# Moving the token-major copy of x from TensorE to VectorE and DMA in a two-layer pooling/SSD trunk

## The chip, the cores and the metric

The kernel runs on one core of one Trainium2 chip. The metric is the device time of one execution in microseconds (us). The kernel before took 1106.39 us, the median of three runs (1106.36 to 1106.46). The engines are TensorE (PE in the rows; PEld is its weight load), VectorE (DVE), ScalarE (ACT), GpSimd (POOL) and SyncE (SP, which issues most DMAs).

## The reference, cut to what matters

The trunk is layer 0 (pooling mixer, then a squared-ReLU MLP) and layer 1 (Mamba-2 SSD mixer, then an MLP), for 512 tokens of width 1024, all float32. The change touches the SSD mixer alone, in the part after the input projection and the causal convolution:

```python
xbc = silu(causal_dwconv(xbc, conv_w, conv_b))      # x: 2048 channels, B and C: 4 groups x 128
dt  = softplus(dt_raw + dt_bias)                    # 32 heads, 8 per group
xdt   = x * dtc[..., None]                          # chunks of 128 tokens, 64 channels per head
a_cs  = cumsum(dtc * a)
decay = exp(where(causal, a_cs[l] - a_cs[s], -inf))
cb    = einsum("bclgn,bcsgn->bcgls", cc, bc)
y_diag = einsum("bcgls,bcgrls,bcsgrp->bclgrp", cb, decay, xdt)
states = einsum("bclgn,bcgrl,bclgrp->bcgrpn", bc, exp(a_cs[-1] - a_cs), xdt)
h[c+1] = h[c] * exp(a_cs[-1]) + states[c]
y_off  = einsum("bclgn,bcgrpn,bcgrl->bclgrp", cc, h, exp(a_cs))
y = y_diag + y_off + d_skip * x                     # then * silu(z), group RMSNorm, out projection
```

The sums over tokens (`y_diag`, `states`) need x with the tokens on the partitions ("token-major"), while the projection and the convolution leave it with channels on the partitions ("feature-major").

## The kernel before

Activations live in SBUF feature-major, as tiles of 128 channels x 512 tokens. Weights come from HBM in units of 128 x 1024 (512 KB). A unit passes four stages. SP loads it into `w_raw` (`load_weights`). ACT rounds it to fp32r as `w_hi` (`round_half`, line 445). POOL subtracts to get `w_lo` (`split_half`, line 729). PE multiplies eight 128x128 tiles with 512 tokens, each as three fp32r products in `three` (lines 857 to 859: hi*hi, hi*lo, lo*hi). Every buffer is doubled, so unit u+2 is rounded and split while unit u is multiplied.

The SSD mixer is a table of "slots", one unit each. Six slots produce the convolved tiles of group 0. Then come ten slots for each group g: t = 0 to 3 compute the gate z of group g, and t = 4 to 9 the convolved tiles of group g+1 (B, C, then four tiles of x). The last group uses its later slots for the output projection. Three PSUM banks take turns as accumulators, so slot a starts only when DVE has drained slot a-3. Between the slots the SSD work of group g is placed by hand:

- After t = 1 `token_major` turns B round (4 transposes, line 1016), makes C*B (line 1025) and turns the x of chunks 0 to 2 round (12 transposes, line 1007). Chunk 3 follows after t = 2 (4 transposes). DVE multiplies each by dt out of PSUM (`token_x`, line 1348).
- After t = 3, 5, 7, 9 `chunk` computes chunks 0 to 3: `y_diag` (line 1048), for chunks 1 to 3 `y_off` (line 1057), and for chunks 0 to 2 the state product `states`, again as three fp32r products.
- ACT forms the exponent of a chunk in `exp_segments` (eight Relus, line 634, and an Exp, line 637), at t = 1, 2, 4, 6. DVE multiplies it by C*B into `m` (`decay_times_cb`, line 1364).
- POOL makes the decayed x (`decayed`, line 788) at t = 2, 4, 6. ACT rounds it (`decayed_hi`, line 626) and POOL takes the rest (`decayed_lo`, line 797). POOL also sums squares of the group before (`group_sum`, line 806).
- The convolution of a tile is `conv_scale` (DVE), `first_tap` (ACT) and three taps on DVE (`conv_taps`, line 1278).

The order on each engine is the order of the code; semaphores tie the engines together. The per-head cumulated sums a_cs go through a DRAM scratch once (line 383) and come back broadcast to 128 partitions, one chunk at a time (`load_acs`), all on the SP queue.

Of the kernel before, what the change touches and what calls it, by code (L numbers as in the profile page):

```python
# [6 lines left out]
F32 = mybir.dt.float32  # L7
# [4 lines left out]
P = 128  # L12
# [44 lines left out]
T_TOKEN, T_LATE_TOKEN = 1, 2  # L57
# [37 lines left out]
def build(nc, xt, x_tok, pooling, weights, dt_weights, params, consts, out_first, out_second):  # L95
    ctx = ExitStack()
    with ctx:
# [52 lines left out]
        bt_hi, _ = sb("b_token_hi", [P, CHUNKS, P], F32R)  # L150
        bt_hi_f = bt_hi[:, :, :].bitcast(F32)
        cbm, _ = sb("cb_masked", [P, CHUNKS, P])
        dec, o_dec = sb("x_dt_decayed", [P, TOK])
        dec_lo, _ = sb("x_dt_decayed_lo", [P, TOK], F32R, o_dec)
        dec_hi, _ = sb("x_dt_decayed_hi", [P, TOK], F32R)
        dec_hi_f = dec_hi[:, :].bitcast(F32)
# [7 lines left out]
        ex, o_ex = sb("dt_exp", hd4)  # L164
# [5 lines left out]
        bt_lo, _ = sb("b_token_lo", [P, CHUNKS - 1, P], F32R, o_ex)  # L170
# [18 lines left out]
        acs_dram = nc.dram_tensor("acs_scratch", [GROUPS, CHUNKS, HPG, P], F32).ap()  # L189
        eacs_dram = nc.dram_tensor("eacs_scratch", [GROUPS, CHUNKS, HPG, P], F32).ap()  # L190
# [5 lines left out]
        XT_BANK = (b_yd, b_yo, b_st, b_misc)  # L196
# [60 lines left out]
        x_mm = sem("x_transposed")  # L257
# [3 lines left out]
        bt_lo_ready = sem("b_token_lo_ready")  # L261
        dec_ready = sem("dec_ready")
        dec_hi_ready = sem("dec_hi_ready")
        dec_lo_ready = sem("dec_lo_ready")
# [59 lines left out]

        def conv_out(n):

            g, q = divmod(n, CONVS)
            return bf[:, :] if q == 0 else cf[:, g % 2, :] if q == 1 else xact[:, q - 2, :]
# [5 lines left out]
        def _(sp):  # L334
# [42 lines left out]
            for u in range(5):  # L377
                load_ahead(u)
            sp.wait_ge(acsf_ready, 1)
# [6 lines left out]
            load_ahead(5)  # L386
            sp.wait_ge(scratch, 2 * GROUPS * 16)
# [44 lines left out]
        def _(act):  # L432
# [142 lines left out]

            for u in range(CONVS):
# [5 lines left out]
                if u == 5:  # L582
# [4 lines left out]
                    act.activation(eacs_f[:, :], acs_f[:, :], ACT.Exp).then_inc(decays, 1)  # L587
                first_tap(u)
# [6 lines left out]
            def silu_b_c(g):  # L595

                for q in range(2):
# [3 lines left out]
            def silu_x(g):  # L601
                act.wait_ge(acc_drained, A_SSM + conv_slot(CONVS * g + CONVS - 1) + 1)
                act.activation(xact[:, :, :], xact[:, :, :], ACT.Silu).then_inc(x_act, 1)

            def skip(g):

                act.wait_ge(x_act, g + 1)
# [10 lines left out]
            def b_token(g):  # L618
                act.wait_ge(bt_mm, g + 1)
                act.activation(bt_hi[:, :, :], b_misc[:, :].rearrange("p (c n) -> p c n", c=CHUNKS),  # L620
                               ACT.Copy).then_inc(bt_ready, 1)

            def decayed_hi(g, c):

                act.wait_ge(dec_ready, 3 * g + c + 1)
                act.activation(dec_hi[:, :], dec[:, :], ACT.Copy).then_inc(dec_hi_ready, 1)
# [29 lines left out]
            for g in range(GROUPS):  # L656
                ends = g == GROUPS - 1
                for t in range(slots(g)):
                    u = slot_of(g, t)
                    if t == 2:  # L660
                        decayed_hi(g, 0)
                    ahead(u, 0)
                    if t == 0:
                        silu_b_c(g)
                        silu_x(g)
# [11 lines left out]
                    if t in (4, 6):  # L677
                        decayed_hi(g, (t - 2) // 2)
                    if not ends and t >= GT:
                        first_tap(CONVS * (g + 1) + t - GT)  # L680
                    if t == 0:
                        skip(g)
                    if t == 1 and g:
# [5 lines left out]
                    if t in FALL_IN:  # L689
# [32 lines left out]
        def _(pool):  # L722
# [60 lines left out]
            def decayed(g, c):  # L783

                pool.wait_ge(xdt_ready, 4 * g + c + 1)
                if g or c:
                    pool.wait_ge(st_ready, 3 * g + c)
                pool.tensor_tensor(
                    dec[:, :].rearrange("p (h d) -> p h d", h=HPG),
# [3 lines left out]

            def decayed_lo(g, c):

# [857 lines left out]
```

## Time and profile before

| | before |
|---|---|
| median of three runs | 1106.39 us |
| profiled execution, its own time | 1106.54 us |
| profiled execution, first to last instruction (span) | 1104.7 us |
| PE busy | 1092.8 us (99%) |
| PE weight loads | 899.8 us (81%) |
| DVE, ACT, POOL busy | 577.3, 474.2, 610.8 us |
| granted TensorE clock | 0.998 of full |
| mean DMA traffic | 106 GB/s |

The busy time of an engine covers the whole span, and a matmul's end is modelled: successive matmuls overlap in the rows. So what a matmul costs is read as the distance from its start to the start of the next one. The SSD part runs from about 386 us to 700 us in the trace.

### The profile page before, as it was taken

The numbers are of one execution on the slowest core, as the hardware profiler recorded it, in microseconds if no ns is written. First come the engines' busy times: TensorE is split into PE (matmuls) and PEld (weight loads), VectorE is DVE, ScalarE is ACT, GpSimd is POOL, SyncE is SP. The second block draws the span as 40 slices with busy tenths as digits, with TensorE's granted clock in tenths as the row PEclk, the third lists the DMA queues.
The fourth block names the chain that finished last, engine by engine and source line by source line (L and its number), as shares of the span: only waits on it lengthen the run. The fifth ranks groups of instructions, "written<-read, shape, count | busy, mean of one in ns | idle before, by whom it ended". The sixth has DMA issues, their size and how long they took to land.

```text
span 1104.7 us, 15384 instructions
## 1 busy us (share of the span) xinstructions
PE 1092.8 (99%) x5168; PEld 899.8 (81%) x5168; DVE 577.3 (52%) x644; ACT 474.2 (43%) x816; POOL 610.8 (55%) x460
## 2 busy tenths in 40 slices
PE   9999999999999999999999999999999999999997
PEld 7788888888888788888887888888888888888886
DVE  5665421455432384676777866666664124554123
ACT  7433222233333338458595785343332222333332
POOL 3866544444566635537466376656665444445653
PEclk9999999999999999999999999999999999999999
DMA  7223232222222225333334233222222222333232
GB/s 286 79 99 105 86 103 97 96 95 95 96 95 95 96 77 152 123 112 124 117 104 143 105 125 106 96 95 96 95 95 96 95 95 95 97 99 101 93 104 77
DMA packets 40085, 117.05 MB, mean 106 GB/s; under 512 B 4080, under 2 KB 11888, under 8 KB 40048
## 3 DMA queue, kind: packets, MB, share of 16 engines
q1 hardware_dynamic: 39616, 115.83, 31.3%
q10 hardware_dynamic: 432, 0.73, 0.2%
q8 instruction: 22, 0.36, 0.1%
q14 instruction: 15, 0.12, 0.0%
HBM read 114.32 MB, written 2.23 MB: 105 GB/s over the span
## 4 chain that ended last, share of the span: by engine, by line
PE 93%; ACT 2%; DVE 1%; POOL 1%; issue 1%; DMA 1%; ACTq 0%; DVEq 0%; POOLq 0%
PE bank L857 30%; PE bank L859 29%; PE bank L858 29%; PE bank L1048 1%; PE bank L1057 1%; DMA params<-params 1%; ACT m L634 1%; PE bank L898 1%; PE bank L1007 0%; ACT w_hi L445 0%; POOL w_lo L729 0%; POOL residual L756 0%; PE bank L878 0%; PE bank L1025 0%; ACT y_accumulated L609 0%
## 5 line engine op out<-in xcount | busy, mean ns | idle before, releaser
L729 POOL TENSOR_TENSOR w_lo<-w_raw,w_hi 128x512 fp32r<-128x512 f32 x372 | 497.5, 1343 | 442.5 <-ACT w_hi L445 429.9
L445 ACT ACTIVATE w_hi<-w_raw 128x512 fp32r<-128x512 f32 x372 | 230.5, 626 | 383.0 <-PE bank L859 373.5
L857 PE MATMUL bank<-x_hi,w_hi 128*128 128x512 f32 x848 | 331.9, 391 | 1.8 <-DVE x_lo L1159 1.5
L859 PE MATMUL bank<-x_hi,w_lo 128*128 128x512 f32 x848 | 330.2, 389 | 0.0
L858 PE MATMUL bank<-x_lo,w_hi 128*128 128x512 f32 x848 | 330.1, 389 | 0.0
L857 PE MATMUL bank<-act_hi,w_hi 128*128 128x512 f32 (+1 forms) x656 | 252.9, 386 | 0.0
L859 PE MATMUL bank<-act_hi,w_lo 128*128 128x512 f32 (+1 forms) x656 | 251.8, 384 | 0.0
L858 PE MATMUL bank<-act_lo,w_hi 128*128 128x512 f32 (+1 forms) x656 | 251.8, 384 | 0.0
L857 PEld LDWEIGHTS bank<-x_hi,w_hi 128*128 128x128 f32 x848 | 159.2, 188 | 37.5 <-issue 2.8
L859 PEld LDWEIGHTS bank<-x_hi,w_lo 128*128 128x128 f32 x848 | 159.2, 188 | 33.1
L858 PEld LDWEIGHTS bank<-x_lo,w_hi 128*128 128x128 f32 x848 | 159.3, 188 | 32.6
L857 PEld LDWEIGHTS bank<-act_hi,w_hi 128*128 128x128 f32 x656 | 123.3, 188 | 24.9 <-POOL w_lo L729 0.5
L858 PEld LDWEIGHTS bank<-act_lo,w_hi 128*128 128x128 f32 x656 | 123.3, 188 | 24.8 <-issue 0.5
L859 PEld LDWEIGHTS bank<-act_hi,w_lo 128*128 128x128 f32 x656 | 123.2, 188 | 24.3
L1246 DVE TENSOR_TENSOR tmp<-bank,rstd 128x512 f32<-128x512 f32 x30 | 20.8, 692 | 223.8 <-PE bank L859 223.8
L1231 DVE TENSOR_TENSOR tmp<-tmp 128x512 f32<-128x512 f32 x64 | 115.4, 1804 | 2.2
L548 ACT ACTIVATE act_hi<-tmp 128x512 f32 x64 | 40.5, 632 | 122.6 <-DVE tmp L1231 122.6
L1228 DVE TENSOR_SCALAR tmp<-bank 128x512 f32<-128x512 f32 x64 | 44.3, 692 | 82.5 <-PE bank L859 82.5
L1235 DVE TENSOR_TENSOR act_lo<-tmp,act_hi 128x512 f32 x64 | 46.0, 719 | 60.0 <-ACT act_hi L548 60.0
L745 POOL TENSOR_TENSOR square_sum<-square_sum,squares 128x512 f32<-128x512 f32 x31 | 47.8, 1542 | 32.5 <-ACT squares L452 32.5
L1249 DVE TENSOR_TENSOR residual<-residual,tmp 128x512 f32 x30 | 51.1, 1703 | 4.6 <-DVE tmp L1246 2.4
L1278 DVE SCALAR_TENSOR_TENSOR x_conv<-bank,params,x_conv 128x511 f32<-128x511 f32 (+2 forms) x48 | 35.9, 749 | 18.8 <-ACT x_conv L572 17.7
(161 smaller groups left out, 725.8 us busy)
## 6 DMA issues: line engine op xcount, KB each, us to landing
w_raw<-weights SPq DMA_DIRECT2D x186, 512.0 KB, 3.3
m<-acs_scratch SPq DMA_DIRECT2D x16, 512.0 KB, 4.4
decay_in<-eacs_scratch SPq DMA_DIRECT2D x24, 128.0 KB, 3.8
x_token<-x_tok SPq DMA_DIRECT2D x4, 512.0 KB, 6.4
residual<-xt SPq DMA_DIRECT2D x8, 256.0 KB, 10.1
out_first<-scaled_residual SPq DMA_DIRECT2D x4, 256.0 KB, 2.4
out_second<-output_rows SPq DMA_DIRECT2D x4, 256.0 KB, 2.7
pooling_matrices<-pooling ACTq DMA_DIRECT2D x2, 288.0 KB, 5.2
```

The costliest lines, as they stand in the source:

```text
L445: act.activation(whi[:, c % 2, part], raw[:, c % 2, part], ACT.Copy).then_inc(hi_ready, 1)
L548: act.activation(act_hi[:, bass.ds(2 * i + e, 1), :], tmp[:, e:e + 1, :], ACT.Copy).then_inc(hid_hi_ready, 1)
L729: pool.tensor_tensor(wlo[:, c % 2, part], raw[:, c % 2, part], whi_f[:, c % 2, part], ALU.subtract).then_inc(lo_ready, 1)
L745: pool.tensor_tensor(ssq[:, :], ssq[:, :], sq[:, slot, :], ALU.add).then_inc(ssq_added, 1)
L857: pe.matmul(out, wh, xh, start=start, stop=False)
L858: pe.matmul(out, wh, xl, start=False, stop=False)
L859: return pe.matmul(out, wl, xh, start=False, stop=stop)
L1228: dve.tensor_scalar(tmp[:, e, :], acc[(a - a0 + first) % 2][:, :], 0.0, None, ALU.max).then_inc(acc_drained, 1)
L1231: dve.tensor_tensor(tmp[:, e, :], tmp[:, e, :], tmp[:, e, :], ALU.mult).then_inc(hid_sq_ready, 1)
L1235: dve.tensor_tensor(act_lo[:, tile, :], tmp[:, e:e + 1, :], act_hi_f[:, tile, :], ALU.subtract).then_inc(hid_lo_ready, 1)
L1249: dve.tensor_tensor(h[:, tile, :], h[:, tile, :], tmp[:, e:e + 1, :], ALU.add).then_inc(h_done, 1)
L1278: dve.scalar_tensor_tensor(out=out[:, back:], in0=p[:, 0:TOK - back], scalar=col("conv_w", 24 * k + n), in1=out[:, back:], op0=ALU.mult, o ...
```

## The change

Five things change.

1. x becomes token-major without PE. DVE transposes 32x32 blocks of the four activated x tiles (`transpose_blocks`, four instructions per group) into the free part of `y_accumulated`. SP writes them to a DRAM scratch in four DMAs (`write_blocks`) and reads them back in one (`read_tokens`). DVE multiplies by dt from there in two halves per chunk (`token_x`). PE's 16 transposes of x per group, and the waits around them, are gone.
2. The state product is one plain float32 matmul of `b_token` and `x_dt_decayed`. `decayed_hi` (ACT), `decayed_lo` (POOL) and `b_token_lo` (DVE) are gone, and the decayed x has two buffers.
3. The convolved tiles come in the order x, B, C. The Silu of x moves to t = 8 of the group before (for group 0 to the fifth of the first six slots), that of B and C stays at t = 0. `skip` moves from t = 0 to t = 3.
4. ACT's exponent of chunk 0 stands in front of `group_squares`.
5. DVE's x_dt and m of chunk 0 stand in front of the gate's drain at t = 2. Those of chunks 1 to 3 follow it.

The diff, cut:

```diff
-        dec, o_dec = sb("x_dt_decayed", [P, TOK])
...
+        dec, _ = sb("x_dt_decayed", [P, 2, TOK])
+        x_dram = nc.dram_tensor("x_scratch", [GROUPS, CHUNKS * (P // Q), Q, P // Q, GT * Q], F32).ap()
...
+            def write_blocks(g):
+                sp.wait_ge(xt_blocks, g + 1)
+                blocks = x_blocks(g)
+                for a in range(P // Q):
+                    sp.dma_start(x_dram[g, :, :, a, :].rearrange("n q f -> q n f"),
+                                 blocks[Q * a:Q * a + Q, :, :]).then_inc(xt_written, 16)
+            def read_tokens(g):
+                sp.wait_ge(xt_written, 16 * (P // Q) * (g + 1))
+                sp.dma_start(yx[:, GT * g:GT * g + GT, :],
+                             x_dram[g].rearrange("(c b) q a f -> (b q) c (a f)", c=CHUNKS)
+                             ).then_inc(xt_landed, 16)
...
+            write_blocks(0)
             sp.wait_ge(acsf_ready, 1)
             sp.wait_ge(decays, 3)
...
             load_ahead(5)
+            read_tokens(0)
             sp.wait_ge(scratch, 2 * GROUPS * 16)
...
+                    if t == 8 and g + 1 < GROUPS:
+                        write_blocks(g + 1)
+                    if t == 9 and g + 1 < GROUPS:
+                        read_tokens(g + 1)
...
+                if u == 4:
+                    silu_x(0)
...
-                act.wait_ge(x_act, g + 1)
+                act.wait_ge(xdt_ready, 4 * g + 4)
                 for i in range(GT):
...
+                    if not ends and t == 8:
+                        silu_x(g + 1)
                     ahead(u, 0)
...
-            def token_x(g, c):
-                for i in range(GT):
-                    last = pe.transpose(XT_BANK[c][:, P * i:P * i + P], xact[:, i, P * c:P * c + P], ident)
-                last.then_inc(x_mm, 1)
...
-                    three(b_st[:, :], bt_hi[:, c, :], bt_lo[:, c, :], dec_hi[:, :], dec_lo[:, :], True, True
-                          ).then_inc(st_ready, 1)
+                    pe.matmul(b_st[:, :], bt[:, c, :], dec[:, c % 2, :], start=True, stop=True).then_inc(st_ready, 1)
...
+            def transpose_blocks(g):
+                dve.wait_ge(x_act, g + 1)
+                blocks = x_blocks(g)
+                for i in range(GT):
+                    last = dve.transpose(blocks[:, :, Q * i:Q * i + Q],
+                                         xact[:, i, :].rearrange("p (n j) -> p n j", j=Q))
+                last.then_inc(xt_blocks, 1)
...
                 conv_scale(u)
+                if u == 4:
+                    transpose_blocks(0)
                 conv_taps(u)
...
+                dve.wait_ge(xt_landed, 16 * (g + 1))
+                out = xdt[:, c, :].rearrange("p (i h a j) -> p h i a j", h=2, a=2, j=Q)
+                landed = yx[:, GT * g + c, :].rearrange("p (h a i j) -> p h i a j", h=2, a=2, j=Q)
+                dt = dt_t[:, c, HPG * g:HPG * g + HPG].rearrange("p (i h) -> p h i", h=2)
+                for half in range(2):
+                    last = dve.tensor_tensor(out[:, half], landed[:, half],
+                                             dt[:, half].unsqueeze(2).unsqueeze(3).to_broadcast([P, GT, 2, Q]),
+                                             ALU.mult)
```

The order of ACT (names: `m` holds the exponents, `squares` the squares of the group before, `x_dt_decayed_hi` the rounded decayed x), from the Silu at t = 0 of group 2 on. Before:

```order
L599 ACTIVATE b_feature<-b_feature 128x512
L599 ACTIVATE c_feature<-c_feature 128x512
L603 ACTIVATE x_conv<-x_conv 128x2048
L616 ACTIVATE z_silu<-z_silu 128x2048
L445 ACTIVATE w_hi<-w_raw 128x512
L609 ACTIVATE y_accumulated<-x_conv,params 128x512 x4
L445 ACTIVATE w_hi<-w_raw 128x512 x2
L642 ACTIVATE squares<-y_accumulated 128x512 x4
L620 ACTIVATE b_token_hi<-bank 128x512
L634 ACTIVATE m<-m,cumulated 128x128 x8
```

And now, the same place:

```order
L625 ACTIVATE b_feature<-b_feature 128x512
L625 ACTIVATE c_feature<-c_feature 128x512
L638 ACTIVATE z_silu<-z_silu 128x2048
L465 ACTIVATE w_hi<-w_raw 128x512 x3
L651 ACTIVATE m<-m,cumulated 128x128 x8
L654 ACT_TABLE_LOAD
L654 ACTIVATE m<-m 128x1024
L659 ACTIVATE squares<-y_accumulated 128x512 x4
L642 ACTIVATE b_token<-bank 128x512
```

The Silu of x and the four skip products have left this place, and the exponent stands ahead of the squares.

The order of POOL at t = 2 of group 1 to 3 (`square_sum` is the sum over the group before, `x_dt_decayed` the decayed x of a chunk). Before:

```order
L788 TENSOR_TENSOR x_dt_decayed<-x_dt,decay_to_end 128x512
L806 TENSOR_TENSOR square_sum<-squares 128x512
L806 TENSOR_TENSOR square_sum<-square_sum,squares 128x512 x2
L797 TENSOR_TENSOR x_dt_decayed_lo<-x_dt_decayed,x_dt_decayed_hi 128x512
L729 TENSOR_TENSOR w_lo<-w_raw,w_hi 128x512 x3
```

And now:

```order
L817 TENSOR_TENSOR square_sum<-squares 128x512
L817 TENSOR_TENSOR square_sum<-square_sum,squares 128x512 x2
L745 TENSOR_TENSOR w_lo<-w_raw,w_hi 128x512
L804 TENSOR_TENSOR x_dt_decayed<-x_dt,decay_to_end 128x512
L745 TENSOR_TENSOR w_lo<-w_raw,w_hi 128x512
```

The decayed x of chunk 0 now stands behind the three sums and a half of a weight unit.

The order of the SP queue at the start of group 0 (`m` and `decay_in` are the broadcast loads of the exponents, `x_scratch` is the new DRAM scratch) is now:

```order
L338 DMA w_raw<-weights 128x1024 x5
L363 DMA x_scratch<-y_accumulated 32x16x128 x4
L398 DMA acs_scratch<-a_cs_feature 8x4x128
L398 DMA eacs_scratch<-exp_a_cs_feature 8x4x128
...
L338 DMA w_raw<-weights 128x1024
L369 DMA y_accumulated<-x_scratch 128x4x512
L345 DMA m<-acs_scratch 128x1024 x2
L355 DMA decay_in<-eacs_scratch 64x4x128 x4
```

Before, the rows with `x_scratch` were not there; now the loads of `m` stand behind the writes and the read of x.

## Rows read from the trace of the kernel before

**Rows 1.** The page: busy time of each engine, share of the span, instructions.

```profile
PE 1092.8 (99%) x5168; PEld 899.8 (81%) x5168; DVE 577.3 (52%) x644; ACT 474.2 (43%) x816; POOL 610.8 (55%) x460
```

**Rows 2.** Waits of PE: engine, line, releaser; us in total, times, longest.

```profile
PE bank L1048 <- DVE m L1364: 1.0, 1, 1.0
```

**Rows 3.** Timeline of PE after t = 1 of group 0: start, duration, instruction.

```profile
429.44 1.47 PE L1007 MATMUL bank<-constants,x_conv 128*128 128x128 f32 x12
430.67 0.48 PE L857 MATMUL bank<-x_hi,w_hi 128*128 128x512 f32 x1
```

**Rows 4.** Timeline of PE at chunk 0 of group 0.

```profile
442.24 1.09 PE L1048 MATMUL bank<-m,x_dt 128*64 128x128 f32 x16
443.26 0.50 PE L857 MATMUL bank<-x_dt_decayed_hi,b_token_hi 128*128 128x512 f32 x1
...
443.83 0.39 PE L859 MATMUL bank<-x_dt_decayed_hi,b_token_lo 128*128 128x512 f32 x1
444.06 0.40 PE L857 MATMUL bank<-x_hi,w_hi 128*128 128x512 f32 x1
444.30 0.39 PE L858 MATMUL bank<-x_lo,w_hi 128*128 128x512 f32 x1
```

**Rows 5.** Timeline of PE at a plain float32 product of the same shape.

```profile
116.68 1.02 PE L878 MATMUL bank<-square_sum,constants 128*128 128x512 f32 x2
117.77 0.39 PE L858 MATMUL bank<-act_lo,w_hi 128*128 128x512 f32 x1
```

**Rows 6.** The chain that ended last, around that product: start, us, what.

```profile
116.84 0.86 PE bank L878 x2
```

**Rows 7.** Timeline of ACT, t = 0 to 2 of group 2.

```profile
559.71 1.90 ACT L603 ACTIVATE x_conv<-x_conv 128x2048 f32<-128x2048 f32 x1
563.83 2.56 ACT L609 ACTIVATE y_accumulated<-x_conv,params 128x512 f32<-128x512 f32 x4
567.33 2.18 ACT L642 ACTIVATE squares<-y_accumulated 128x512 f32<-128x512 f32 x4
569.89 2.44 ACT L634 ACTIVATE m<-m,cumulated 128x128 f32<-128x128 f32 x8
572.35 1.28 ACT L637 ACT_TABLE_LOAD   x1
573.64 1.06 ACT L637 ACTIVATE m<-m 128x1024 f32<-128x1024 f32 x1
```

**Rows 8.** Timeline of ACT, t = 4 of group 2.

```profile
587.38 0.63 ACT L626 ACTIVATE x_dt_decayed_hi<-x_dt_decayed 128x512 fp32r<-128x512 f32 x1 [2.01 <-POOL x_dt_decayed L788]
```

**Rows 9.** Timeline of DVE before group 0: taps of the fourth convolved tile.

```profile
411.53 2.32 DVE L1278 SCALAR_TENSOR_TENSOR x_conv<-bank,params,x_conv 128x511 f32<-128x511 f32 x3 [0.84 <-ACT x_conv L572]
```

**Rows 10.** Timeline of SP at the start of group 0.

```profile
424.45 3.29 SPq L356 DMA_DIRECT2D decay_in<-eacs_scratch  x4
```

**Rows 11.** The page, DMA issues: KB each, median us from issue to landing.

```profile
m<-acs_scratch SPq DMA_DIRECT2D x16, 512.0 KB, 4.4
```

**Rows 12.** Timeline of POOL, t = 2 of group 2.

```profile
570.02 1.05 POOL L788 TENSOR_TENSOR x_dt_decayed<-x_dt,decay_to_end 128x512 f32<-128x512 f32 x1
571.02 1.30 POOL L806 TENSOR_TENSOR square_sum<-squares 128x512 f32<-128x512 f32 x1
572.47 2.73 POOL L806 TENSOR_TENSOR square_sum<-square_sum,squares 128x512 f32<-128x512 f32 x2
```

**Rows 13.** Timeline of PE at chunk 0 of group 2.

```profile
577.26 1.09 PE L1048 MATMUL bank<-m,x_dt 128*64 128x128 f32 x16
```

**Rows 14.** Timeline of DVE, taps of the tile of t = 8, group 2.

```profile
622.31 2.32 DVE L1278 SCALAR_TENSOR_TENSOR x_conv<-bank,params,x_conv 128x511 f32<-128x511 f32 x3 [0.85 <-ACT x_conv L572]
```

**Rows 15.** Timeline of PE, first unit after chunk 3 of group 2.

```profile
621.09 0.48 PE L857 MATMUL bank<-x_hi,w_hi 128*128 128x512 f32 x1
```

**Rows 16.** DVE lines of the SSD part: count, busy us, mean ns, idle before.

```profile
L1348 DVE TENSOR_TENSOR x_dt<-bank,dt_token 128x512 f32<-128x512 f32 x16 | 10.2, 678 | 0.0
```

**Rows 17.** The line of m on DVE: shortest, median and longest duration in ns.

```profile
L1364 DVE TENSOR_TENSOR m<-m,cb_masked x16: 1216/1748/2306, 437.0 to 676.5; 128x1024 f32<-128x1024 f32 x16
```

More of the change, by code:

```diff
@@ L56 @@
 TIMES_CB_IN = {4: 1, 6: 2, 8: 3}
-T_TOKEN, T_LATE_TOKEN = 1, 2
+T_TOKEN = 1
+Q = 32
 T_STAT, T_NORM = 4, 7
@@ L574, in first_tap, with silu_x @@
                                ).then_inc(tap_ready, 1)
+            def silu_x(g):
+                act.wait_ge(acc_drained, A_SSM + conv_slot(CONVS * g + GT - 1) + 1)
+                act.activation(xact[:, :, :], xact[:, :, :], ACT.Silu).then_inc(x_act, 1)
             for u in range(CONVS):
@@ L595, in silu_b_c @@
             def silu_b_c(g):
-                for q in range(2):
+                for q in range(GT, CONVS):
                     act.wait_ge(acc_drained, A_SSM + conv_slot(CONVS * g + q) + 1)
                     act.activation(conv_out(CONVS * g + q), conv_out(CONVS * g + q), ACT.Silu).then_inc(bc_act, 1)
-            def silu_x(g):
-                act.wait_ge(acc_drained, A_SSM + conv_slot(CONVS * g + CONVS - 1) + 1)
-                act.activation(xact[:, :, :], xact[:, :, :], ACT.Silu).then_inc(x_act, 1)
             def skip(g):
-                act.wait_ge(x_act, g + 1)
+                act.wait_ge(xdt_ready, 4 * g + 4)
                 for i in range(GT):
@@ L664, in _ @@
                         silu_b_c(g)
-                        silu_x(g)
                         if g:
@@ L688, in _ @@
                         root(SSM_STAT + g - 1, group_root)
-                    if t in FALL_IN:
+                    if t in FALL_IN and t > 1:
                         exp_segments(g, FALL_IN[t])
@@ L820, in _ @@
                     u = slot_of(g, t)
+                    if t == 2 and g:
+                        group_sum(g - 1)
+                    split_half(U_SSM + u + 2, 0)
                     if t == 2:
                         decayed(g, 0)
-                    if t == 2 and g:
-                        group_sum(g - 1)
-                    if t == 2:
-                        decayed_lo(g, 0)
-                    split_half(U_SSM + u + 2, 0)
-                    if t in (4, 6):
-                        decayed(g, (t - 2) // 2)
                     if t == T_STAT - 1 and g:
@@ L834, in _ @@
                     split_half(U_SSM + u + 2, 1)
-                    if t in (4, 6):
-                        decayed_lo(g, (t - 2) // 2)
+                    if t == 2:
+                        decayed(g, 1)
+                    if CHUNK_AFTER.get(t - 1) == 0:
+                        decayed(g, 2)
                     if g == GROUPS - 1 and t == 10:
@@ L1027, in token_major @@
                 last.then_inc(cb_mm, 1)
-                pe.wait_ge(x_act, g + 1)
-                if g == 0:
-                    pe.wait_ge(acsf_ready, 1)
-                else:
-                    pe.wait_ge(y_add, 4 * g)
-                    pe.wait_ge(y_dec, 3 * g)
-                    pe.wait_ge(state_ready, 3 * g)
-                for c in range(CHUNKS - 1):
-                    token_x(g, c)
             def c_chunk(g, c):
@@ L1044, in chunk @@
                 pe.wait_ge(xdt_ready, 4 * g + c + 1)
-                if c:
+                if g == 0 and c == 0:
+                    pe.wait_ge(acsf_ready, 1)
+                else:
                     pe.wait_ge(y_add, 4 * g + c)
```

86 lines of the change are left out of this document (33 added, 53 removed).

## The prediction

> **What bounds the kernel now.** I read the page's engine times first: TensorE is busy for 1092.8 us, 99% of the span, and no other engine passes 610.8 us [rows 1]. So time goes only where TensorE's own work shrinks or one of its few waits goes, and it comes back wherever a new wait reaches TensorE. Next the waits of TensorE: inside the SSD part there is one of a size that counts, 1.0 us, for DVE's m [rows 2]. It falls at chunk 2 of group 2. Then the timelines of the places that the change touches, for what an instruction costs on TensorE, and those of ACT, POOL, DVE and SP around them, for the slack that the moved work has. The reader is to see in them that matmuls follow each other every 0.23 us (443.83 to 444.06 [rows 4]), so a unit of 24 products is 24 x 0.23 = 5.5 us.
>
> **TensorE's transposes of x.** Twelve in a row take 430.67 - 429.44 = 1.23 us [rows 3], 0.103 us each. Each group has 16, so 1.64 us per group and 4 x 1.64 = 6.6 us in all. They stand on TensorE's own queue, so all of it comes off the path. Leaving and entering fp32r for the four late ones may add 0.1 us.
>
> **The state product, 12 times.** Before, from the first of the three fp32r products to the second product of the next unit: 444.30 - 443.26 = 1.04 us [rows 4]. The plain float32 product of the same shape, to the same point: 117.77 - 116.68 = 1.09 us [rows 5]. That is 0.05 us more. The other side: its two passes take 0.86 us [rows 6] against 3 x 0.23 = 0.69, so 0.17 more. 12 times gives 0.6 to 2.0 us of loss; I take the middle, 1.3, since the one example has a switch of number format at its head that this place doesn't have.
>
> **The old wait.** TensorE's 1.0 us for m [rows 2] was the end of an overloaded ACT: in t = 0 and 1 it did the Silu of x (1.90), the skip products (2.56) and the squares (2.18) ahead of the exponent (2.44 + 1.28 + 1.06) [rows 7], and at t = 4 it stood still 2.01 us until POOL had a decayed x for it to round [rows 8]. That rounding is gone and the exponent is first. I take the 1.0 us as gone. What is late next on that chain is DVE's m itself, and it has at least that microsecond of room.
>
> **ACT, DVE and POOL work that goes** (rounding, remainders) lies beside TensorE and is worth nothing by itself. What is added: four DVE transposes per group. The trace has none; the nearest rows are DVE operations over 512 columns, three taps in 2.32 us, 0.77 each [rows 9], and the product out of PSUM, 0.68 [rows 16]. Lower end 0.6, upper end by the factor that m shows between its shortest and longest case, 2306/1216 = 1.9 [rows 17], so 1.5. I take 0.75, 3.0 us per group.
>
> **New wait 1: the start of group 0.** The chain is now: taps of the fourth tile end at 411.53 + 2.32 = 413.85 [rows 9]. Silu of x 1.90 [rows 7]: 415.8. Four transposes 3.0: 418.8. Four writes of 512 pieces of 512 bytes each: four loads of 256 such pieces took SP 3.29 us [rows 10], so 3.3 to 6.6; I take 5: 423.8. Landing: 4.4 us is the median of a 512 KB load [rows 11], for 256 KB I take 3 (2 to 4.4): 426.8. SP waits for that in front of the read. Behind it stand the read of x (1 MB) and the load of m for chunk 0: 1.0 to issue, 4.4 to land [rows 11], some 3 for the megabyte ahead of it: 435.2. The exponent: 2.44 + 1.28 + 1.06 = 4.8 [rows 7]: 440.0. DVE's m: 1.2 to 2.3, median 1.75 [rows 17]: 441.7. TensorE wants it at 442.24 - 1.64 = 440.6 [rows 4]. So it waits 1.1 us. With the low ends it waits nothing, with the high ends (1.6 + 1.4 + 0.6 more, and 0.75 more for transposes) some 5 us. I take 1.0. The weight unit queued behind the read has the same delay and the same cover.
>
> **New wait 2: chunk 0 of groups 1 to 3.** TensorE's state product there waits for POOL's decayed x. It now stands behind three sums (1.30 + 2.73) and a half unit (about 1.3, as the first sum), then 1.05 for itself [rows 12]. ACT's squares begin about where they did: 4.8 later for the exponent, 1.90 + 2.56 earlier for Silu and skip [rows 7], so at 567.33 + 0.3 = 567.6. The sums can start after two of the four, at 568.7, and POOL is through at 568.7 + 4.0 + 1.3 + 1.05 = 575.1. TensorE gets to it at 577.26 - 1.64 + 1.0 = 576.6 [rows 13]. There is 1.5 us of room. But [rows 17] shows DVE operations that take 1.1 us longer than their like, and if POOL's share such delays three times, the room turns into 1.8 us of wait. I take 0.4 each, 1.2 in all (0 to 5.4).
>
> A rule bears on this. DVE's x_dt was a product out of PSUM, at 0.678 us in the mean and with no idle time [rows 16], while m, with two SBUF inputs, ranges up to 2.3 us [rows 17]. The Trainium skill, "SBUF — State Buffer", section "SBUF: two separate sides", says that a DVE operation with two SBUF inputs and a GpSimd operation lock each other out for the whole instruction. By that rule the trace agrees for m, and the change makes x_dt such an operation too; this is a rival below.
>
> **Cover 3: the tile of t = 8 in groups 1 and 2.** Its taps end at 622.31 + 2.32 = 624.6 [rows 14]. The slot that needs its bank is the second after chunk 3: 621.09 + 5.5 = 626.6 [rows 15]. The room is 2.0 us and the transposes stand ahead of the taps with 3.0. But the old lateness of ACT (2.01 us [rows 8]) that pushed this stretch of DVE is gone, so I cost it at nothing. With transposes of 1.5 us it would be 6.0 - 4.0 = 2.0 us of wait, or 4.0 if ACT's lateness gives nothing back, twice.
>
> **Cover 4: the SP queue in groups 1 to 3.** At t = 8 SP stands until the transposes are done and then issues the writes, at t = 9 it stands until they have landed. Queued behind are the weight unit of t = 9 and the loads of m and decay_in. A unit is rounded two slots after the one that frees its buffer, 11.0 us; less 4.4 to land leaves 6.6 against a delay of about 5. Hidden, with 1.6 us to spare.
>
> **The sum.** -6.6 + 1.3 - 1.0 + 1.0 + 1.2 = -4.1 us. The profiled execution took 1106.54 us by its own time (1104.7 of it span), the median of the runs is 1106.39, the same within 0.15. 1106.4 - 4.1 = 1102.3 us.
>
> A second rule gives another number for new wait 1. The Trainium skill, "DMA: Bandwidth & Descriptors", section "Anatomy of one DMA — SWDGE (gpsimd) path", puts a DMA at about 2.0 us plus its bytes at 436 GB/s. By it a megabyte is 4.4 us each way (an estimate from that page), the chain is some 5 us shorter, TensorE doesn't wait in group 0, and the sum would be 1101.3.
>
> **Rivals.**
> - No new wait. The slack covers everything: -6.6 + 1.3 - 1.0 = -6.3, so 1100.1 us. For it: [rows 12, 13] leave 1.5 us, and both DVE and POOL lose work. Against it: four places would all have to hold, each with under 2 us. Chance 0.2.
> - The way through DRAM is long. Writes in 512-byte pieces issue and land at their high ends, and m of group 0 comes 3 to 4 us later than I take it: 1102.3 + 3.5 = 1105.8 us, within 0.2% of before. For it: four loads of half the pieces held SP for 3.29 us [rows 10]. Against it: x has more than ten microseconds before it is used, and only group 0 has m behind it. Chance 0.15.
> - The shared port. The eight half products of x_dt per group each wait for POOL, and POOL for them, as m does by up to 1.1 us [rows 17]. POOL's decayed x is then late by 1.8 us in three groups, 5.4 instead of 1.2, and m of chunk 0 loses its room too: 1102.3 + 4.2 = 1106.5 us. By the skill's rule above this is the outcome. Against it: the halves of chunks 1 to 3 stand behind the drain, where nobody is near to waiting. Chance 0.1.
> - DVE becomes the bound, the case on the other side. The transposes take 1.5 us each, 6.0 us instead of 3.0 at t = 8, in the stretch where DVE already runs behind TensorE [rows 14, 15]. Then +3.0 at the start of group 0, 4.0 twice at t = 8, and the late B and C and x_dt push chunk 0 by 1.8 instead of 0.4 three times: 3.0 + 8.0 + 4.2 = 15.2, 1102.3 + 15.2 = 1117.5 us. It decides once new waits pass 1.0 + 1.2 + 4.1 = 6.3 us, so with transposes of about 1.1 us already. For it: nothing in this trace has their price. Chance 0.12.
>
> **How the numbers follow.** The forecast has 0.4, the rivals 0.2, 0.15, 0.1 and 0.12; 0.03 is left. 0.2% is 2.2 us, about what a measurement of this kernel can tell from no change: faster is below 1104.2, slower above 1108.6. Faster: 0.37 of the forecast, the 0.2, and 0.11 from the low ends of the next two: 0.68. Same: 0.03 + 0.14 = 0.17 and 0.02 of the last: 0.19. Slower: 0.13. The range runs from 1099.3 (all covers hold and the state product costs only 0.6, -7.0) to 1107.0, which takes in the DRAM and the port cases and leaves out the DVE case.
>
> **What would show it.** TensorE's transposes of x gone and its weight loads 64 fewer. The float32 state product at 0.86 in the chain. The wait of m at chunk 2 of group 2 gone. A wait of the products with m at chunk 0 of group 0 near 1 us, with m's DMA as what ACT waits for. Waits of the state product for POOL's decayed x, 0.4 us each, in groups 1 to 3. DVE's transposes near 0.75 us. The prediction is wrong if a transpose takes over 1.1 us, if TensorE waits for weights behind a standing SP queue, or if the plain state product costs more than 1.1 us from start to next start.

## The result: slower, 1114.52 us

The changed kernel took 1114.52 us in the median of 4 runs (1112.19 to 1115.36), against 1106.38 for the kernel before on the same chip: ratio 1.0070, interval [1.0053, 1.0088]: slower by 0.7%, clear of the noise. The forecast was 1102.3 with a range up to 1107.0. The execution that the profile shows took 1115.36 us, span 1113.6, 8.9 more than the span before.

The page after, busy time by engine, against [rows 1]:

```profile
PE 1092.4 (98%) x5092; PEld 893.3 (80%) x5092; DVE 605.3 (54%) x672; ACT 470.8 (42%) x806; POOL 595.3 (53%) x448
```

TensorE has 76 instructions fewer (64 transposes, and 12 products for which two passes stand in place of three). ACT and POOL have less to do, as they should. DVE has 28.0 us more, where the forecast allowed 4 x 3.0 for transposes.

TensorE's waits in the SSD part after, against the one of [rows 2]:

```profile
PE bank L1061 <- POOL x_dt_decayed L804: 7.1, 4, 3.1
PE bank L1044 <- DVE m L1369: 1.6, 2, 1.0
PE bank L1044 <- DVE y_accumulated L1388: 0.9, 1, 0.9
PE bank L866 <- POOL w_lo L745: 0.4, 1, 0.4
```

TensorE's path can be measured out by landmarks: the first transpose of B in a group (at t = 1) and the first product with m of each chunk, each with its distance to the next. Between the first landmark of group 0 (428.1 before, 428.0 after) and that of chunk 3 of group 3, the change lost 8.95 us:

```
distance                     before, groups 0 to 3         after                         sum of differences
transposes to chunk 0        14.13 14.13 14.12 14.33       12.35 12.32 13.03 12.35       -6.7
chunk 0 to chunk 1           12.80 13.26 13.26 13.26       17.12 13.68 14.76 19.28       +12.3
chunk 1 to chunk 2           13.71 13.71 14.75 13.70       13.89 13.89 15.62 13.89       +1.4
chunk 2 to chunk 3           13.71 13.70 13.74 13.71       13.89 14.02 14.83 13.89       +1.8
chunk 3 to next transposes                                                               +0.2
```

Most is lost between chunk 0 and chunk 1, above all in groups 0 and 3. There TensorE reaches the state product before POOL's decayed x is there. The timeline of TensorE in group 3 (start, duration, instruction, the idle time before it and what ended it), against the unbroken one of [rows 4]:

```profile
653.08 2.08 PE L1061 MATMUL bank<-x_dt_decayed,b_token 128*128 128x512 f32 x2 [3.10 <-POOL x_dt_decayed L804]
654.17 1.42 PE L866 MATMUL bank<-act_hi,w_hi 128*128 128x512 f32 x1
655.38 0.63 PE L867 MATMUL bank<-act_lo,w_hi 128*128 128x512 f32 x1
655.81 0.63 PE L868 MATMUL bank<-act_hi,w_lo 128*128 128x512 f32 x1
...
658.76 0.40 PE L866 MATMUL bank<-act_hi,w_hi 128*128 128x512 f32 x1
```

The wait is 3.10 us, but the distance grew by 6.0. The products behind the wait follow each other every 0.43 us and not every 0.23. The windows of the same stretch (window, length, TensorE's busy time, granted clock, DMA) say why:

```profile
648.00:650.00 2.00, 1.99 (x21) 1.00 0.00 0
650.00:652.00 2.00, 0.00 (x0) 0.97 0.00 0
652.00:654.00 2.00, 0.92 (x1) 0.50 0.00 0
654.00:656.00 2.00, 2.00 (x5) 0.50 0.28 51
656.00:658.00 2.00, 2.00 (x7) 0.50 0.55 211
658.00:660.00 2.00, 2.00 (x9) 0.82 0.00 0
```

TensorE stood still from about 650 on, and the granted clock fell to 0.50, that is from 2.4 to 1.2 GHz, until past 658. From the start of the state product to the tenth product behind it are 658.76 - 653.08 = 5.68 us. The same ten steps without a wait take 3.04 (from the kernel `state_only` below: 1.20 to the second product, then 8 x 0.23), so the low clock cost 2.6 us on top of the 3.10. In group 0 a wait of 2.65 us cost 1.4 more in the same way.

**Group 3, who was late.** POOL and DVE in front of that wait, in the timeline of each:

```profile
645.18 1.60 POOL L817 TENSOR_TENSOR square_sum<-squares 128x512 f32<-128x512 f32 x1 [3.17 <-ACT squares L659]
646.93 3.50 POOL L817 TENSOR_TENSOR square_sum<-square_sum,squares 128x512 f32<-128x512 f32 x2
650.40 1.45 POOL L745 TENSOR_TENSOR w_lo<-w_raw,w_hi 128x512 fp32r<-128x512 f32 x1
651.80 1.23 POOL L804 TENSOR_TENSOR x_dt_decayed<-x_dt,decay_to_end 128x512 f32<-128x512 f32 x1
```

```profile
643.69 0.68 DVE L1439 TENSOR_TENSOR z_silu<-bank,rstd 128x512 f32<-128x512 f32 x1
644.29 0.68 DVE L1345 TENSOR_TENSOR cb_masked<-bank,constants 128x512 f32<-128x512 f32 x1
644.88 0.74 DVE L1358 TENSOR_TENSOR x_dt<-y_accumulated,dt_token 128x256 f32<-128x256 f32 x2
645.55 2.32 DVE L1369 TENSOR_TENSOR m<-m,cb_masked 128x1024 f32<-128x1024 f32 x1
647.79 0.68 DVE L1439 TENSOR_TENSOR z_silu<-bank,rstd 128x512 f32<-128x512 f32 x1
648.39 7.51 DVE L1358 TENSOR_TENSOR x_dt<-y_accumulated,dt_token 128x256 f32<-128x256 f32 x6
```

The first x_dt was ready at 645.6, and TensorE wanted its decayed form at 650. POOL did four other things first. It was slow at the sums, which ran beside DVE's m: 1.60 + 3.50 us, against 1.30 + 2.73 in [rows 12]. And it began them late: the chain that ended last leads from ACT's exponent, in front of the squares, back to a weight load that was queued on SP behind the writes of x and landed after 6.63 us.

```profile
631.48 6.63 DMA w_raw<-weights
...
638.13 1.15 ACT w_hi L465 x2
639.28 2.34 ACT m L651 x8
```

ACT itself stood for that load only 0.88 us. It had stood longer, 1.34, for the convolved C, whose tile now comes last (timeline of ACT; group 2 has the same 1.34 and no wait for weights):

```profile
634.29 0.64 ACT L625 ACTIVATE c_feature<-c_feature 128x512 f32<-128x512 f32 x1 [1.34 <-DVE c_feature L1270]
638.13 1.15 ACT L465 ACTIVATE w_hi<-w_raw 128x512 fp32r<-128x512 f32 x2 [0.88 <-DMA w_raw<-weights]
```

On DVE the six halves of x_dt behind it took 7.51 us, 1.25 each, though the first two, begun while POOL was idle, took 0.74 together. Such a half is what the change put in place of half a product out of PSUM at 0.678 for the whole [rows 16].

**Group 0.** There POOL had nothing in front of the decayed x but the half unit, and that had no weights. The chain that ended last (start, duration, what):

```profile
430.87 9.88 DMA w_raw<-weights
...
440.77 0.64 ACT w_hi L465
...
441.48 1.39 POOL w_lo L745
442.87 1.19 POOL x_dt_decayed L804
...
444.10 2.07 PE bank L1061 x2
```

while the x_dt that it needed had been ready for nine microseconds when POOL took it up at 442.87 (timeline of DVE):

```profile
432.79 0.76 DVE L1358 TENSOR_TENSOR x_dt<-y_accumulated,dt_token 128x256 f32<-128x256 f32 x2 [2.57 <-DMA y_accumulated<-x_scratch]
438.91 1.23 DVE L1369 TENSOR_TENSOR m<-m,cb_masked 128x1024 f32<-128x1024 f32 x1 [5.36 <-ACT m L654]
```

### The profile page after: what moved, and what is told of

It is laid out like the page before. It is cut to its first block, busy times and chain, and to the rows that moved or that the text cites. A ratio compares the mean times of both kernels' runs of the same rounds, so it can differ in the third digit from the quotient of the medians.

```text
span 1113.6 us, 15250 instructions
## 1 busy us (share of the span) xinstructions
PE 1092.4 (98%) x5092; PEld 893.3 (80%) x5092; DVE 605.3 (54%) x672; ACT 470.8 (42%) x806; POOL 595.3 (53%) x448
## 4 chain that ended last, share of the span: by engine, by line
PE 79%; DVE 7%; ACT 5%; POOL 4%; DMA 3%; issue 2%; SPq 1%; DVEq 0%; ACTq 0%; POOLq 0%
PE bank L866 25%; PE bank L868 25%; PE bank L867 25%; DMA w_raw<-weights 2%; DVE x_conv L1270 1%; POOL w_lo L745 1%; ACT m L651 1%; POOL square_sum L817 1%; ACT w_hi L465 1%; PE bank L1061 1%; PE bank L1053 1%; ACT x_conv L592 1%; DMA params<-params 1%; DVE y_accumulated L1280 1%; PE bank L1044 1%
## 5 line engine op out<-in xcount | busy, mean ns | idle before, releaser
L866 PE MATMUL bank<-x_hi,w_hi 128*128 128x512 f32 x848 | 336.0, 396 | 2.1 <-DVE x_lo L1151 1.5
```

The lines of the kernel that those rows point to most:

```text
L866: pe.matmul(out, wh, xh, start=start, stop=False)
```

## The experiments

Times are medians; ratios are to the kernel before, run on the same chip.

**1. One half of the change: `state_only`.** The kernel before with the plain float32 state product; x keeps its transposes and all orders stay.

```diff
-  three(b_st, bt_hi[:, c], bt_lo[:, c], dec_hi, dec_lo, True, True)
+  pe.matmul(b_st, bt[:, c], dec, start=True, stop=True)
```

> The kernel before with only the state product changed to one plain float32 product; rounding and remainders of the decayed x and of B are gone. Theory A (the plain product itself is cheap, the loss comes from the way x goes): TensorE pays 12 x 0.17 = 2.0 us, and gets back the old wait of 1.0 us for m, since ACT no longer waits for POOL at t = 4: 1106.4 + 1.0 = 1107.4, between 1106.4 and 1107.8. Rival B (the plain product sits on the path in a way the starts don't show, for instance it waits for POOL's decayed x by itself): waits of over 0.5 us at chunk 0 and 1109 or more.

1107.13 us (10 runs), ratio 1.0006 [0.9997, 1.0016], as theory A had it. Each distance with a state product grew by 0.18, and no wait is left in the SSD part: the m of [rows 2] was in time. TensorE at chunk 0 of group 0, to be read against [rows 4]:

```profile
442.81 1.12 PE L1042 MATMUL bank<-x_dt_decayed,b_token 128*128 128x512 f32 x2
443.38 0.80 PE L834 MATMUL bank<-x_hi,w_hi 128*128 128x512 f32 x1
444.01 0.39 PE L835 MATMUL bank<-x_lo,w_hi 128*128 128x512 f32 x1
```

From its start to the second product behind it: 1.20 us, against 1.04 before. So this half isn't what lost 8 us.

**2. The other half: `x_path_only`.** The changed kernel, but the state product in its three parts again, with the rounding on ACT and the remainders on DVE and POOL. Decayed x has one buffer again, and that of chunks 1 and 2 is formed at t = 4 and 6 as before the change.

> The changed kernel with the state product as three fp32r products again (with the rounding on ACT and the remainders on POOL and DVE). Theory A (x through DVE and DRAM loses by what it makes late: DVE's halves of x_dt, POOL's decayed x): the wait of the state product at chunk 0 stays or grows, since rounding and remainder come behind it, 1114 to 1122. Rival B (the plain product carries the loss): under 1110.

1124.71 us (4 runs), ratio 1.0164 [1.0147, 1.0181]: worse than either theory. Its waits for the remainder of decayed x, and its halves of x_dt (count, busy, mean ns, idle before):

```profile
PE bank L890 <- POOL x_dt_decayed_lo L830: 16.8, 4, 5.8
```

```profile
L1383 DVE TENSOR_TENSOR x_dt<-y_accumulated,dt_token 128x256 f32<-128x256 f32 x32 | 34.9, 1148 | 2.8 <-DMA y_accumulated<-x_scratch 2.8
```

So the plain product didn't cause the loss. The loss is in the x path and the orders, and it sits on the way to decayed x, which is two steps longer here; why this run is 10 us worse than the change is not taken apart further.

**3. POOL's order: `dec_before_half`.** Decayed x of chunk 0 in front of the half unit, still behind the sums.

```diff
+  if t == 2: decayed(g, 0)
   split_half(U_SSM + u + 2, 0)
-  if t == 2: decayed(g, 0)
```

> The changed kernel with POOL's decayed x of chunk 0 put in front of the half weight unit at t = 2 (still behind the three sums). Theory A (the wait of 7.1 us is POOL's order): in group 0 the 2.65 us wait falls to what the weight unit behind its DMA costs, about 0.7; in group 3 from 3.1 to 1.6 plus 0.5 for the half unit, in group 2 from 1.2 to 0.4; with the time at the lower clock that follows two of the waits, 4 to 6 us less: 1108.5 to 1110.5. Rival B (the late thing is the whole chain ahead of POOL, so the wait moves to the weight half): the sum of the waits for decayed x and w_lo stays within 1.5 us of 7.5, and the time above 1112.

1108.15 us (10 runs), ratio 1.0017 [1.0007, 1.0027]: 6.4 us of the 8.1 lost come back by swapping two operations, a little more than was expected. No wait for decayed x is left, chunk 0 to chunk 1 is 13.55, 13.45, 13.99 and 13.98. What is left is

```profile
PE bank L1044 <- DVE m L1369: 2.5, 3, 1.0
PE bank L866 <- POOL w_lo L745: 1.8, 3, 1.2
PE bank L1044 <- DVE y_accumulated L1388: 1.4, 2, 0.9
```

**4. The halves of x_dt: `dt_from_psum`.** The factor of x_dt is read from PSUM, so that the product has one input in SBUF, as before the change. The bank is that of C times B, so the values are not dt: this kernel leaves dt out of x_dt. It also has two more semaphore waits on TensorE, which keep that bank until x_dt has read it; its trace shows no time lost at them.

```diff
-  dt = dt_t[:, c, HPG * g:HPG * g + HPG].rearrange("p (i h) -> p h i", h=2)
+  dt = b_stat[:, P * c:P * c + HPG].rearrange("p (i h) -> p h i", h=2)
```

> The changed kernel with DVE's x_dt multiplied by values from a PSUM bank (C times B) in place of dt: the values are others, the shapes and the order are the same, and the operation has one SBUF input in place of two. Theory A (the two SBUF inputs lock out POOL and are locked out by it): the 32 halves fall from 1.07 us in the mean to about 0.4, DVE is 20 us less busy, POOL's w_lo beside them gets shorter, and the time falls by 1 to 4 us. Rival B (the halves are long for another reason, such as the strides of the four-dimensional access): they stay at 0.8 us or more.

1108.88 us (7 runs), ratio 1.0022 [1.0011, 1.0034]: 5.6 us come back, where at most 4 were expected. The halves, against 32.4 us and 1072 ns each in the changed kernel:

```profile
L1360 DVE TENSOR_TENSOR x_dt<-y_accumulated,bank 128x256 f32<-128x256 f32 x32 | 11.2, 411 | 2.7 <-DMA y_accumulated<-x_scratch 2.7
```

The waits for m and y_accumulated are gone, only POOL's is left (5.7 us, 3 times: 2.08, 2.46 and 1.20 in groups 0, 2 and 3). Here ACT stood for late weights in group 2 and not in group 3, and it is group 2 that has the long wait:

```profile
566.00 1.15 ACT L465 ACTIVATE w_hi<-w_raw 128x512 fp32r<-128x512 f32 x2 [0.94 <-DMA w_raw<-weights]
```

So the m of chunk 2 of group 2, the old wait, came back in the changed kernel through the slow halves.

**5. Both: `both_causes`.** The true dt this time, which ACT copies into the PSUM bank of token-major B once it has drained that (0.28 us a group).

> The change with both remedies in one: the first decayed x in front of the half unit, and dt read by x_dt from PSUM, here with its true values, which ACT copies there behind token-major B (one copy of 128x128 a group). Alone they gave 1108.15 and 1108.88. Theory (two separate causes, GpSimd's order and the slow halves of x_dt): their gains overlap at chunk 0, where both shorten the same wait, and add up elsewhere, where the waits for m (2.5 us), for the sum y_accumulated (1.4 us) are the halves' doing alone and the wait for decayed x (5.7 us) the order's alone: 1104.0 (1103.0 to 1105.5). Rival (one cause seen twice, both only pull decayed x forward): no better than the better of the two, 1107.5 to 1108.5.

1106.10 us (11 runs), ratio 0.9996 [0.9987, 1.0005]. Together they bring 8.4 us, alone 6.4 and 5.6: they overlap, as both shorten the way to decayed x. It is 2 us more than was expected. One cause of that is a wait that this kernel brings along: DVE waits for ACT's copy, which stands behind the exponent, and m of group 0 is late for it.

```profile
PE bank L1049 <- DVE m L1375: 1.4, 1, 1.4
```

**6. SP's order: `both_and_sp`.** As 5, with the decay_in loads behind the first weight load of group 0.

> As both_causes, and the two decay_in loads in front of group 0 go behind the first weight load of group 0 in SP's queue. Theory (in group 0 the weight load stands behind x's DMAs and decay_in and lands late, 9.9 us after its issue, so that w_hi and w_lo are late and TensorE waits up to 1.2 us for w_lo): 0.8 to 1.5 us less than both_causes, 1102.9 (1101.8 to 1104.3). Rival (the load is slow since the 1 MB read of x shares the engines with it, wherever it stands): the same as both_causes within 0.3 us. Second rival (decay_in then comes late for chunk 1): slower than both_causes by 0.5 or more.

1106.58 us (11 runs), ratio 0.9998 [0.9989, 1.0007]: nothing, where 0.8 to 1.5 us were expected. This sooner place in SP's queue isn't worth anything once the decayed x doesn't wait for those weights.

**7. ACT's order: `exp_behind_squares`.** The changed kernel with the first exponent behind the squares again.

> The change with ACT's order of before: the first exponent behind the squares and token-major B again. Theory (at chunk 0 of groups 1 to 3 the sums of squares and m come off the same queue of ACT, so whichever is second is late): the wait for decayed x of group 3 goes, since the squares and the sums run 4 us sooner, and one for m of 3 us takes its place: 1114.5 (1112.5 to 1117). Rival (m had slack of several us there): the wait goes and nothing takes its place, 1110 to 1112. Rival 2 (both are late, as squares in front also lengthen DVE): over 1117.

1115.90 us (4 runs), ratio 1.0082 [1.0066, 1.0097], like the change itself. Transposes to chunk 0 are now 14.42 and 14.41 in groups 2 and 3, with waits for m of up to 2.0, and chunk 0 to chunk 1 of group 3 fell from 19.28 to 16.36. One late thing was traded for another, so this part of the change neither lost nor won. Groups 2 and 3 have the same pair of waits here, 2.00 us for m and 1.23 for decayed x behind it. In group 2 the granted clock stayed at 1.00, and chunk 0 to chunk 1 took 14.74; in group 3 it fell to 0.50, and the same stretch took 16.36.

**8. POOL's order of before: `dec_before_sums`.** Decayed x in front of the sums too.

> The change with GpSimd's order of before for the first decayed x: in front of the three sums and of the half unit. Theory (GpSimd's order is the larger cause; moreover GpSimd then waits for the first x_dt, and is idle while DVE makes it, so that its two halves are quick): no wait for decayed x at all, a bit better than behind the sums (1108.15): 1107.5 (1106.5 to 1108.7). Rival (sums and half unit that now wait for x_dt come late: TensorE waits for w_lo or for the group statistic): 1109 to 1112.

1107.67 us (11 runs), ratio 1.0011 [1.0002, 1.0020]. The first theory's time, with part of the rival: no wait for decayed x, but w_lo is late by 1.98 in group 2, since the sums now stand between. The clock fell to 0.50 behind that wait, and chunk 0 to chunk 1 took 17.28. A wait of 1.92 at the same place of group 3 left the clock at 1.00, and there it took 15.59.

**9 to 11. Three more orders.** `b_first` is a version built to remove every wait of chunk 0: token-major B and the copy of dt in front of the exponent, and on POOL decayed x, one sum, the half unit, two sums. `b_first_sbuf` is the same with dt from SBUF. `b_first_half` puts the half unit and the first sum in front of decayed x.

> A version built on the findings. x_dt takes dt from PSUM as in both_causes; ACT makes token-major B and the copy of dt in front of the first exponent (in both_causes they stood behind the squares, so that DVE waited 1.4 to 2.0 us for the copy in groups 2 and 3 and until 439.8 in group 0); GpSimd does decayed x of chunk 0 first of all, then one sum of squares, the first half unit, the other two sums. Theory (all that the change lost was waits of chunk 0): no wait for decayed x, m or w_lo at any chunk 0, distances 12.33 and 13.45 in every group, 66.5 us a group against 67.3 to 69.0 before: 1101.5 (1099.8 to 1103.5). Rival (ACT's 0.9 us in front of the exponent makes m late): waits for m of up to 1 us a group, 1103.5 to 1106.

> As b_first, but dt is read from SBUF as in the change itself: what the slow halves of x_dt cost once the order is right. Theory (6 halves of 1.25 us in place of 0.34 delay only what DVE does behind them, the state and the sums): chunk 0 is as in b_first, groups 1 to 3 lose 1 to 2 us each at chunks 1 and 2: 3 us over b_first, 1104.5 (1103 to 1106.5). Rival (the order was all, the halves are hidden): within 0.7 us of b_first.

> b_first with GpSimd's order at t = 2 turned once more: one sum of squares, the first half unit, decayed x of chunk 0, the other two sums, the second half unit. In b_first GpSimd was idle 3.7 us for the first x_dt in groups 2 and 3, and w_lo and the sum's remainder were late by 0.4 to 0.6 us each (waits of 0.9, 1.1 and 0.7 us in all, and the distances of chunk 0 of groups 2 and 3 at 15.08 and 14.94 against 13.44 in group 1). Theory (each short wait costs its own length and some more while TensorE fills up again): these waits go, chunk 0 of groups 2 and 3 falls to 13.5 to 14: 1104.0 (1102.8 to 1105.3). Rival (half units, sums and decayed x fill GpSimd so that one of them is late in any order): another wait comes in their place, 1105.8 to 1107.

They gave 1106.26 (0.9998 [0.9989, 1.0007]), 1108.13 (1.0015 [1.0006, 1.0024]) and 1109.91 us (1.0027 [1.0018, 1.0036]). All three missed their theory by 3.6 to 5.9 us. In `b_first` group 1 has the distances that were expected (12.33, 13.44, 13.89, 13.89), but groups 2 and 3 have short waits, for w_lo (0.9), the sum's remainder (1.1), y_accumulated (0.9), the residual (0.7) and m (0.4). The slow halves cost 1.9 us even in this order. `b_first_half` was a mistake in group 0: there the half unit has no weights until 440.2, and everything behind it on POOL waits:

```profile
443.27 1.12 PE L1068 MATMUL bank<-x_dt_decayed,b_token 128*128 128x512 f32 x2 [1.89 <-POOL x_dt_decayed L808]
```

```profile
444.00:446.00 2.00, 2.00 (x7) 0.68 0.26 45
446.00:448.00 2.00, 2.00 (x6) 0.50 0.63 221
```

Its chunk 0 to chunk 1 in group 0 is 16.57 against 13.31 in `b_first`: 3.26 us for a wait of 1.89, with the clock down again. In groups 2 and 3 it won nothing (15.00 and 14.95 against 15.08 and 14.94), so the wait only moved from one of POOL's results to another, as the rival said.

**12. The best version: `both_g0_first`.** `both_causes`, and in group 0 alone token-major B and the copy of dt in front of the exponent, where ACT waits for a DMA anyway.

```diff
+  if t == T_TOKEN and g == 0: b_token(g)
   if t == 1: exp_segments(g, FALL_IN[t])
   if t == 1 and g: group_squares(g - 1)
-  if t == T_TOKEN: b_token(g)
+  if t == T_TOKEN and g: b_token(g)
```

> both_causes (1106.1), and in group 0 alone ACT makes token-major B and the copy of dt in front of the first exponent, while it waits for m's DMA anyway; in groups 1 to 3 nothing is moved. Theory (in group 0 of both_causes DVE waited for the copy until 439.8, m was late, TensorE waited 1.4 us; b_first showed no wait there): group 0 gains 1.4 us, the rest stays: 1104.7 (1103.9 to 1105.6), faster than before. Rival (the groups behind shift against the DMAs and lose it again): 1105.7 to 1106.6.

1104.59 us (1103.84 to 1105.37, 11 runs), ratio 0.9984 [0.9975, 0.9993]: faster than the kernel before by 1.8 us, and than the changed one by 9.9. TensorE still waits a little:

```profile
PE bank L1068 <- POOL x_dt_decayed L810: 1.3, 2, 1.0
PE bank L1051 <- DVE y_accumulated L1396: 1.0, 2, 0.7
PE bank L872 <- POOL w_lo L751: 0.8, 3, 0.5
```

## Why the prediction was wrong, step by step

- **TensorE's transposes of x, -6.6.** Right, if low: the distance to chunk 0 fell by 1.78, 1.81 and 1.98 in groups 0, 1 and 3, and by 1.09 plus a wait of 0.61 for m in group 2: 7.3 us.
- **The state product, +1.3.** Too small: 12 x 0.18 = 2.2 us (`state_only`). From its start to the next product are 0.57 us there (442.81 to 443.38), against 0.46 in the one example of [rows 5]; the product behind it takes 0.63 in both.
- **The old wait, -1.0.** Right for its reason: with ACT's rounding gone the wait went (`state_only`). In the changed kernel it is there again at 1.00, through the halves of x_dt (`dt_from_psum` removes it).
- **DVE's transposes** took 0.60 us each, four in 2.49, not 0.75. The rival "DVE becomes the bound" at 1117.5 was near in time and wrong in its mechanism.
- **New wait 1, the start of group 0, 1.0.** The chain to m was right to a few tenths or pessimistic: the exponent began at 434.05 for a forecast of 435.2, m was there at 440.1, no wait. (The high end was added up wrongly: transposes of 1.5 us are 3.0 more for the four, not 0.75. The forecast didn't rest on it.) What failed is the sentence that the weight unit behind the read "has the same delay and the same cover". It landed 9.88 us after its issue, and what it had in front of TensorE wasn't its own unit but the decayed x queued behind its half on POOL. 2.65 us of wait and 1.4 at the low clock: 4.1.
- **New wait 2, chunk 0 of groups 1 to 3, 1.2.** The step that failed most. Measured 0.16, 1.23 and 3.10, and 2.6 more in group 3 from the clock: 7.1 us. Its room of 1.5 us was counted from squares at 567.6, "4.8 later for the exponent, 1.90 + 2.56 earlier", that is 4.5 behind the first transpose of the group (563.14). They began 5.5, 6.5 and 7.4 behind it in groups 1, 2 and 3: the sum moved ACT's work about and left out that ACT has to wait itself. In groups 2 and 3 it waited for the convolved C (1.34 us), in group 3 also for the weights (0.88). POOL's first sum in group 3 stood idle for the squares until 645.18, 8.6 behind the first transpose for a forecast of 5.6 (568.7 less 563.14). From there to the end of decayed x POOL took 7.9 us (to 653.03) for a forecast of 6.4, the sums being slow beside m. So 3.1 late and 1.5 longer, less the room of 1.5, is the wait of 3.1. Putting the exponent back behind the squares didn't help (`exp_behind_squares`). No run takes the wait for C away, so its share is read from the trace and not shown by an experiment.
- **Cover 3** held: behind the transposes (at 625.9 in group 2) TensorE waited for no bank, and chunk 3 to the next transposes grew by 0.2 us in all. The wait of 0.9 for y_accumulated comes before them, at 623.4, and goes with the slow halves (`dt_from_psum`).
- **Cover 4** failed in group 3 though TensorE never waited for those weights: it was counted against the rounding that TensorE needs, "hidden, with 1.6 us to spare", but ACT stands at a late rounding with its whole queue, the exponent and the squares, and so POOL's sums and decayed x. It stood 0.88 us. The decayed x was late by 3.10 there and by 1.23 in group 2, where the weights were in time; in `dt_from_psum` the two groups changed places, with 2.46 where ACT stood 0.94 and 1.20 where it didn't. It is the mistake of group 0 once more.
- **The shared port**, a rival with chance 0.1 and 1106.5 us, was a main cause: 5.6 us when taken away alone. What argued against it, that the late halves stand where nobody waits, was wrong: DVE had no gap behind them, and the copies of the state, m and y were pushed on.
- **Nothing in the sum stood for TensorE's clock.** Every wait was priced at its length. The two long ones cost 5.75 us of wait and 4.0 us at 1.2 GHz. Of the four runs one had a mean granted clock of 0.997 where the others had 0.993; it took 1112.19 us, they 1114.50 to 1115.36.

Summed up: -7.3 for the transposes, +2.2 for the state product, +7.1 for decayed x, +4.0 for the clock, and +0.6, +0.9 and +0.4 for m, y_accumulated and w_lo make +7.9. The landmarks show +8.95. The last microsecond isn't assigned to a wait. 0.4 of it lies between chunks 0 and 1, where the distances grew by 4.4 beyond the waits and the 0.18 for the product, and not by 4.0; no run here settles the rest.

The rule of the Trainium skill that the prediction cited, "SBUF — State Buffer", section "SBUF: two separate sides", speaks of a full lock between DVE with two SBUF inputs and GpSimd. By that rule, these traces agree in kind: with both inputs in SBUF a half takes 0.37 us while POOL is idle and 1.25 while it works, with one input in PSUM 0.34 to 0.37 either way. The other rule of the Trainium skill that was cited, "DMA: Bandwidth & Descriptors", section "Anatomy of one DMA — SWDGE (gpsimd) path", a DMA at 2.0 us and its bytes at 436 GB/s, gave 4.4 us for a megabyte as an estimate. The section is about DMAs that GpSimd issues, these are issued by SP, and the read took 7.2 us in the median here. TensorE waited in group 0 all the same, for decayed x and not for m.

## What to carry to other kernels

When an operation moves behind others on its queue, look at what the first of those waits for, in each stage apart: in group 0 a half unit without weights held up a product whose input had been ready for nine microseconds. Before a product out of PSUM is turned into one out of SBUF, price it at the rate that it has beside a busy GpSimd, and count what stands behind it. And where TensorE is the bound, price a new wait of two or three microseconds at more than its length. In the changed kernel the two longest cost half as much to nearly as much again at the low clock, and the single waits of 1.23 us and less cost no more than 0.1 beyond themselves. It can't be read from the length alone: of two waits of 1.98 and 1.92 us in one trace the clock fell behind the first only. A late weight load is to be priced by everything queued behind the instruction that waits for it, not by its own use.

## What the runs showed of the hardware

- After idle stretches of 1.89 us (`b_first_half`), 2.65 and 3.10 us (the changed kernel) TensorE's granted clock was 0.50 of 2.4 GHz, and products followed each other at 0.43 us instead of 0.23. The excess over the wait was 1.4, 1.4 and 2.6 us. The wait of 1.23 us in group 2 cost 0.1 over its length.
- The length of the wait doesn't settle it. In `exp_behind_squares` 2.00 + 1.23 us of waits kept the clock at 1.00 in group 2 and were followed by 0.50 in group 3; in `dec_before_sums` 1.98 us were followed by 0.50 and 1.92 us were not.
- A half product x_dt (128x256, strided, float32): 0.37 us with POOL idle, 1.25 beside it. POOL pays as well: decayed x takes 1.04 us alone and 1.22 beside such halves.
- DVE's transpose in blocks of 32, 128x512 float32: one every 0.60 us, the same as a product of that size out of PSUM.
- Transfers in 512-byte pieces: writes of 256 KB landed after 4.5 us, and a weight load that normally lands in 3.3 us took 9.88 behind them and the megabyte's read.
